# A hybrid decoder step: who makes the low halves of the weights, a new order of the mixer steps, and gate rows spread in one pass

## The reference

```python
u = _rmsnorm(h, w['norm1_g']) @ w['w_in']           # all mixer inputs in one product
y_a, ... = _rglru(a_x, a_g, ...)                    # causal conv, two sigmoid gates, linear recurrence
y_b = _swa_prompt(q, k, v, w['attn_sinks'])         # window of 128; a cached version for the samples
y_c, ... = _hgrn2(c_q, c_f, c_i, c_g, lb, s0, ...)  # chunks of 64, decay for every key channel
y_d, ... = _mlstm(d_q, d_k, d_v, d_o, d_i, d_f, ...)  # chunks of 64, gates of one number a head
h = h + jnp.concatenate([y_a, y_b, y_c, y_d], axis=-1) @ w['w_out']
f = _rmsnorm(h, w['norm2_g']) @ w['w_up']
h = h + jnp.square(jax.nn.relu(f)) @ w['w_down']
h = h + jax.nn.sigmoid(h @ w['w_ple_gate']) * (p_l @ w['w_ple_proj'])
```

## Time and profile before

| | us |
|---|---|
| median of 3 runs | 2978.51 |
| lowest, highest | 2973.07, 2979.11 |
| the profiled execution | 2969.13 |
| its span in the profile | 2966.9 |
| TensorE busy | 2818.4 (95%) |
| GpSimd busy | 1440.4 (49%) |
| VectorE busy | 1347.5 (45%) |
| ScalarE busy | 1114.2 (38%) |
| mean granted clock of TensorE | 0.975 |

### The profile page before, as it was taken

One profiled execution on the slowest core, in us unless ns is written; L12 is line 12 of the kernel. 1 busy time (PEld: TensorE's weight loads), 2 busy tenths in 40 slices (PEclk: granted clock), 3 DMA queues, 4 the chain that ended last, 5 costly groups with the idle time before them and its releaser, 6 DMA issues.

```text
span 2966.9 us, 43775 instructions
## 1 busy us (share of the span) xinstructions
PE 2818.4 (95%) x17944; PEld 2495.7 (84%) x17944; DVE 1347.5 (45%) x2398; ACT 1114.2 (38%) x1728; POOL 1440.4 (49%) x896
## 2 busy tenths in 40 slices
PE   7998998899989999999999899999999999999998
PEld 6878776677867898989998887878789779999998
DVE  6647346556645545435442266544453423222222
ACT  5442334542333444433332344533333243322222
POOL 3336333445734744446642554434664265555453
PEclk9999999999999999999998999999999899999999
DMA  4322222332232432222222242323222234233232
GB/s 163 111 86 65 86 73 78 109 104 82 79 102 80 136 106 79 85 78 85 81 80 63 72 150 79 107 66 100 85 85 81 65 91 153 93 93 93 92 94 86
DMA packets 85717, 274.20 MB, mean 92 GB/s; under 512 B 9994, under 2 KB 10762, under 8 KB 85520
## 3 DMA queue, kind: packets, MB, share of 16 engines
q1 hardware_dynamic: 71312, 243.23, 26.3%
q10 hardware_dynamic: 14208, 28.18, 2.7%
HBM read 251.31 MB, written 20.06 MB: 91 GB/s over the span
## 4 chain that ended last, share of the span: by engine, by line
PE 78%; DVE 6%; POOL 4%; ACT 3%; issue 2%; DMA 1%; ACTq 0%; SPq 0%; DVEq 0%; POOLq 0%
PE pj L644 23%; PE pj L646 23%; PE pj L645 23%; POOL w_lo L1559 2%; DVE sl L1656 2%; PE pm L728 1%; PE pm L912 1%; POOL m_lo L1629 1%; ACT w_hi L1072 1%; PE pm L993 1%; DMA out_y<-res 1%; PE pm L1012 1%; PE pm L820 1%; DVE wide L2091 0%; PE pm L832 0%
## 5 line engine op out<-in xcount | busy, mean ns | idle before, releaser
L1559 POOL TENSOR_TENSOR w_lo<-w_raw,w_hi 128x1024 fp32r<-128x1024 f32 x428 | 1051.3, 2460 | 1038.5 <-ACT w_hi L1072 1038.0
L644 PE MATMUL pj<-m_hi,w_hi 128*128 128x260 f32 (+1 forms) x2320 | 748.0, 322 | 18.1 <-POOL w_lo L1559 7.5
L646 PE MATMUL pj<-m_hi,w_lo 128*128 128x260 f32 (+1 forms) x2320 | 732.6, 316 | 0.0
L645 PE MATMUL pj<-m_lo,w_hi 128*128 128x260 f32 (+1 forms) x2320 | 732.3, 316 | 0.0
L644 PE MATMUL pj<-hid,w_hi 128*128 128x260 f32 (+1 forms) x1920 | 631.0, 329 | 21.0 <-POOL hid L1622 9.9
L646 PE MATMUL pj<-hid,w_lo 128*128 128x260 f32 (+1 forms) x1920 | 622.3, 324 | 0.0
L1072 ACT ACTIVATE w_hi<-w_raw 128x1024 fp32r<-128x1024 f32 x428 | 447.7, 1051 | 394.9 <-PE pj L646 373.7
L645 PE MATMUL pj<-hid,w_hi 128*128 128x260 f32 (+1 forms) x1536 | 496.6, 323 | 0.0
L644 PEld LDWEIGHTS pj<-m_hi,w_hi 128*128 128x128 f32 x2320 | 442.4, 191 | 55.5 <-POOL w_lo L1559 12.9
L645 PEld LDWEIGHTS pj<-m_lo,w_hi 128*128 128x128 f32 x2320 | 441.7, 190 | 31.5 <-issue 3.4
L646 PEld LDWEIGHTS pj<-m_hi,w_lo 128*128 128x128 f32 x2320 | 441.7, 190 | 28.8
(11 more groups left out here) (318 smaller groups left out, 3254.4 us busy)
## 6 DMA issues: line engine op xcount, KB each, us to landing
w_raw<-in_w SPq DMA_DIRECT2D x428, 512.0 KB, 3.5
out_e<-stage SPq DMA_DIRECT2D x23, 260.0 KB, 3.8
sl<-out_e SPq DMA_DIRECT2D x23, 260.0 KB, 4.0
out_y<-res ACTq DMA_DIRECT2D x16, 260.0 KB, 4.6
out_y<-res ACTq DMA_DIRECT2D x16, 256.0 KB, 4.6
x_b<-in_x SPq DMA_DIRECT2D x4, 520.0 KB, 13.7
res<-in_x ACTq DMA_DIRECT2D x8, 260.0 KB, 4.7
res<-out_y ACTq DMA_DIRECT2D x8, 260.0 KB, 5.4
```

What stands on the lines that cost most here:

```text
L644: pe.matmul(out, wh, hi[:, k, c0:c1], start=(k == 0), stop=False)
L645: pe.matmul(out, wh, lo[:, k, c0:c1], start=False, stop=False)
L646: last = pe.matmul(out, wl, hi[:, k, c0:c1], start=False, stop=(k == n - 1))
L1559: pool.tensor_tensor(w_lo[:, j % RAW_BUFS, :], w_raw[:, j % RAW_BUFS, :], w_hi[:, j % HI_BUFS, :].bitcast(F32), ALU.subtract).then_inc(lo_ ...
```

## The change

1. **Low parts.** Of the 428 tiles, 390 get their `w_lo` on VectorE and 38 on GpSimd (the 32 tiles of `wout`, and three after `gates` in q = 2 and 3). `lo_made` becomes two semaphores, one per engine.
2. **hgrn levels.** `q_diag` is dropped; the levels are multiplied in place, six operations a chunk on VectorE instead of twelve, and every level is four products of K = 64.
3. **Rows and conv of pass 1** are done beside the output products of pass 0 (`BESIDE`), with slots of their own; their loads come earlier. The reciprocal is replaced by a short polynomial on VectorE.
4. **Steps.** A gate step becomes two (one for each half of the channels), so there are four in a pass; `hdiag` comes after both `hprep` 2 and 3 and in pass 0 has two dense steps of the next pass ahead of it; one `AFTER` entry moves from `mc` 0 to `mc` 3. `_sequence` now holds products back until dense steps worth 1.0 have passed (`down` counts 0.5).
5. **vt** uses another PSUM bank for v = 2 and 4; the table of `rope` is loaded after the step's products.
6. **Gate rows in `mc`.** VectorE writes the rounded rows to partitions 64 to 67 and the remainder to 96 to 99 of `grow`; one F32R product over 36 partitions with a selector `gsel` spreads their sum.

The core of the diff:

```diff
@@ _sequence
+        if late and x[0] not in ('sq', 'resid'):
+            out, held, late = out + held, [], False
...
         elif x[0] in DENSE:
-            out, held = out + [(x, 'dense')] + held, []
+            out.append((x, 'dense'))
+            passed += 0.5 if x[0] == 'down' else 1.0
+            late = passed >= 1.0
         else:
-            out, held = out + held + [(x, 'pre')], []
+            out, held, passed = out + held + [(x, 'pre')], [], 0.0
@@ which engine makes a low part
+    by_pool = {JOBS[x][0] for x in JOBS if x[0] == 'wout'}
+    for q in (2, 3):
+        first = JOBS[('job', q, 'gates')][0]
+        by_pool |= set(range(first + 2, first + 5))
@@ vector, at the end of each dense step
+                    dve.wait_ge(hi_made, j + 1)
+                    dve.tensor_tensor(w_lo[:, j % RAW_BUFS, :], w_raw[:, j % RAW_BUFS, :],
+                                      w_hi[:, j % HI_BUFS, :].bitcast(F32), ALU.subtract).then_inc(lo_made[0], 1)
...
+                if part == 'dense':
+                    split_lo(JOBS[x][-1] + 3)
@@ rows
-                    link(dve.tensor_scalar(t2, t2, -1.0, 1e-30, ALU.add, ALU.max))
-                    link(dve.reciprocal(t2, t2))
+                    link(dve.tensor_scalar(t2, t2, -0.5, 1.5, ALU.mult, ALU.add))
+                    link(tt(f, f, t2, ALU.mult))
+                    link(tt(ln, ln, f, ALU.subtract))
...
+                    link(dve.tensor_copy(f[:, 0:HALF].bitcast(F32R), ig[:, 0:HALF]))
+                    dve.tensor_copy(grow[64:68, 0:HALF], ig[:, 0:HALF])
+                    dve.tensor_tensor(grow[96:100, 0:HALF], ig[:, 0:HALF], f[:, 0:HALF], ALU.subtract).then_inc(rows_v, 1)
@@ mc, tensor
-                        last = pe.matmul(pm[:, 0, i * CH:(i + 1) * CH], ident[0:4, head:head + 1].to_broadcast([4, P]),
-                                         rows8[0:4, cc], start=False, stop=(i == 3), skip_group_check=True)
+                        last = pe.matmul(pm[:, 0, i * CH:(i + 1) * CH], gsel[64:100, head:head + 1].to_broadcast([36, P]),
+                                         grow[64:100, cc], start=False, stop=(i == 3), skip_group_check=True)
@@ hP, tensor: every level
-                            if l < 6:
-                                out = pm[:, bank + j, :].rearrange("p (h s) -> p h s", h=2)[:, :, at:at + 64]
-                                last = pe.matmul(out, el[:, j, :], q_diag[:, l % 4, j], start=True, stop=True)
-                                continue
                             for hh in range(2):
                                 r = slice(64 * hh, 64 * hh + 64)
-                                last = pe.matmul(pm[:, bank + hh, j * 256 + at:j * 256 + at + 64], el[r, j, :],
-                                                 el[r, j, half:], start=True, stop=True)
+                                last = pe.matmul(pm[:, bank + hh, j * 256 + at:j * 256 + at + 64], el[r, j, :], odd[r, j],
+                                                 start=True, stop=True)
```

More of the change, by code:

```diff
@@ L81, in mixer @@
     if ahead:
-        o = take(q, 'gates', 'ag0', 'ag1') + [('rows', q, 0), ('rows', q, 1)]
+        o = [('rowsT', q)] + take(q, 'ag0', 'ag1')
     else:
@@ L156, in blend @@
     return out + ff
-AFTER = {('rows', 1): 2, ('conv', 0, 1): 2, ('conv', 1, 1): 2, ('gate', 0): 1, ('gate', 1): 1, ('rows', 5): 2, ('lru', 1): 2,
+AFTER = {('rows', 1): 2, ('hdiag',): 2, ('conv', 1, 1): 2, ('gate', 0, 1): 1, ('gate', 1, 1): 1, ('rows', 5): 2, ('lru', 1): 2,
          ('rowsT',): 2, ('rope', 2): 2, ('ropeE', 1): 1, ('rot', 0): 1, ('rot', 2): 1, ('attn', 0): 2, ('attn', 1): 2,
@@ L179, in _order @@
     for q in range(4):
-        ahead = [('load', 1, 'ax0'), ('load', 1, 'ax1')] + [('conv', 1, j, n) for j in range(2) for n in range(2)]
         for n in range(KT):
-            o += [('wout', q, n)] + ([ahead[n]] if q == 0 and n < 6 else [])
-        o += blend(mixer(q + 1), feed(q), 3) if q < 3 else feed(q)
+            o += [('wout', q, n)] + (BESIDE[n] if q == 0 else [])
+        ff = feed(q)
+        first = ff.index(('up', q, 0, 2)) if q == 0 else 0
+        o += ff[:first] + blend(mixer(q + 1), ff[first:], 3) if q < 3 else ff
         o += [('pload', q)]
@@ L194, in _sequence @@
 def _sequence():
-    out, held = [], []
+    out, held, passed, late = [], [], 0.0, False
     for x in ORDER:
+        if late and x[0] not in ('sq', 'resid'):
+            out, held, late = out + held, [], False
         if x[0] in AUX:
@@ L244, in _tables @@
         if part == 'pe':
[L245 to L253, removed]
+            if what in ('gate', 'gnorm', 'rope', 'rot', 'norm1', 'norm2'):
+                for name in [x + (i,) for i in range(2)] if what == 'gnorm' else [x]:
+                    mixes[name] = m
+                    m += n
     return shot, job, used_until, mixes
@@ L758, in gate @@
             def gate(x):
[L759 to L762, removed]
+                q, g, j = x[1:]
+                pe.wait_ge(conv_v, 2 * q + j + 1)
+                mix(MIX[x], q, pc(q // 2, 'wr' if g == 0 else 'wi', j * P, P), slot(11 + j))
             def rope(x):
@@ L1176, in gate @@
             def gate(x):
[L1177 to L1180 removed]
+                q, g, j = x[1:]
+                take_mix(MIX[x], q, slot(13 + 2 * g + j), ACT.Sigmoid, bias=pc(q // 2, 'br' if g == 0 else 'bi', j))
             def lru(x):
@@ L2000, in hprep @@
                     last.then_inc(hp_v, 1)
-            def diagonal(lev, qs):
-                for hh in range(2):
-                    r = slice(64 * hh, 64 * hh + 64)
-                    last = tt(q_diag[r, lev % 4, :, hh, :].rearrange("p j (n b) -> p j n b", b=1 << lev),
-                              halves(level(lev)[r], lev)[1], halves(qs[r], lev)[1], ALU.mult)
-                return last
             def hE(x):
@@ L2032, in hE @@
                     dve.wait_ge(hc_exp, 3 * n + g)
-                    for lev in ((0, 1), (2, 3))[g - 1]:
-                        last = diagonal(lev, qs)
+                    for lev in GROUPS[g - 1]:
+                        e1 = halves(level(lev), lev)[1]
+                        last = tt(e1, e1, halves(qs, lev)[1], ALU.mult)
                     last.then_inc(hc_kq, 1)
```

147 lines of the change are left out of this document (90 added, 57 removed).

## The result

| | before | with the change |
|---|---|---|
| median, us | 2975.79 (4 runs) | 2952.88 (4 runs) |
| lowest, highest | 2972.55, 2979.11 | 2949.51, 2957.22 |
| the profiled execution, its span | 2969.13, 2966.9 | 2952.48, 2950.7 |

The direction and the range held; the gain is less than half of the forecast one.

A forecast was written before the change was run, and what follows sets the result against it. TensorE's matmuls were taken as the floor (busy 2818.4 of 2966.9 us). Gains of 71.5 less costs of 26 gave net -45.5: 2923.6 from the profiled execution, 2933 from the median, middle 2928; range 2878 to 2971.

The forecast's parts named there:

- The low parts: 390 of 428 low parts move from GpSimd to VectorE: 11 us less of TensorE's waits for w_lo.
- the price of VectorE's queue: VectorE, working in order, makes low parts late for the next dense tile: three waits, +8 us (0 to 25).
- The slow rival: VectorE's in-order queue is late with low parts, so TensorE waits for w_lo: slower, 3012 us; chance 0.10.
- The rival of the shared path: VectorE and GpSimd still hold each other up on shared memory access: only 9 us gained, 2969; chance 0.14.
- gates, hdiag and vt: TensorE's waits in gate steps, hdiag and vt shrink by reordering and another PSUM bank: -12, -6 and -3 us.
- four new waits: Last half's hdiag, sattn and rope lack a dense product between preparation and products: about 2 us each, +8 (0 to 16).
- The hgrn waits: Waits for VectorE's copies in the hgrn levels (13.8 + 4.7 us) halve as its work is less stretched: -9 (0 to -18).
- The products of the levels: In the hgrn levels, four K = 64 products replace pairs of K = 128: +5 us over 96 levels (-1 to +14).
- The spread: Spreading the gate rows in one F32R pass saves about 0.45 us, 16 times: -7 us (-9 to 0).
- The rows beside the output products: Some 22 row operations, about 16 us, on VectorE beside the first output products barely fit: +5 us (0 to 12).
- Hid: TensorE's waits for hid, 9.9 us, left unchanged because GpSimd had waited for ScalarE's hsq, not for a low part.
- The clock: Four half-clock stretches at hdiag, gate and m_lo waits end when those waits go: -13 us (0 to -19).

## Why the prediction was wrong in size

*The low parts: right on the engines, and the step that failed is the price of VectorE's queue.* GpSimd's 518 us and VectorE's 1568 fit, and so does the 1.27 us; m_lo fell by 2.7 of the forecast 5, mden and stage by 3.0 of 5.5. The forecast put the cost of the in-order queue where the low part is needed, at the next dense tile (+8, "with all of the next mixer step behind it"), and left attention at nothing, "since they end on ScalarE or on a chain within the step". The move by itself did not lengthen the waits for w_lo: 15.9 us in the kernel with the low parts alone, where the terms come to 15. But VectorE is a part of that chain within the attention step, at the place shown it has no gap, and a low part that it makes there delays the chain, by up to its own length. The attention waits rose from 13.1 to 20.2 us, and to 27.5 with the low parts alone; the runs with and without those 30 or 32 tiles give 14 and 24 us.

*The slow rival named the right queue, but not the right wait.* It priced VectorE's queue in waits for w_lo; what was late was the attention's work behind the low part. In the kernel with the low parts alone this took back the whole gain: ratio 1.0. The rival of the shared path falls: moving 390 low parts is worth 14 us in the new order and, without the attention's, 24 in the old one. The page of the Trainium skill that was cited for it ("Perfetto Trace Analysis", section "Optimizing Scalar/DVE Operations") says "might not help"; the engines do collide here (2.77 against 0.75 us), but the move did help, in the old order as long as the attention's stayed on GpSimd. It took most of the collisions away: with the low parts alone VectorE is busy 1620.1 us, where its 1347.5 before and the 495.5 of the 390 low parts add to 1843, so 223 us of its other work were stretching.

*Order: gates, hdiag and vt came near the forecast; the rope step was priced far too low.* The sigmoid line fell by 11.5 (forecast 12), less 1.9 that now wait in the gate step for the conv; hdiag by 4.5 (6), its longest wait growing from 3.0 to 4.1; vt from 3.7 to 1.0 (3). The forecast had the rope step among four new waits of about 2 us (+8, 0 to 16), for want of a dense product in between. The issue of the rope table behind the loads was in the diff, and had no term: +14.4 us of waits, 18 with the clock. The waits for w_lo that did grow in the changed kernel came with the order as well, 8.0 us of them at the first output products and the `up` step behind them.

*The hgrn waits* fell by 11.8 (9 forecast), but in the new order not through the relief, as the run with all low parts on GpSimd shows; the prediction had the multiplication in place "off the path". The products of the levels cost about 2 us more over all chunks by the starts of their steps, within the bounds of +5. *The spread* gave 9.8 us directly, where the forecast had 7, and 9 with the low clock counted; in all it was worth 20 with what went through the clock. *The rows beside the output products* cost 9, within 0 to 12 and by the late evictions that were named.

*Hid* was left at 9.9 and fell to 2.4. It stands at 9.9 with the low parts alone, at 2.4 with all of them on GpSimd in the new order, and at 12.5 with the old rule for held products: the rule did it. *Two lines without a term* grew: evictions (`res`) from 4.5 to 7.3, and the mLSTM chunks' wait for `wide` (L1044) from 4.3 to 8.3. Both are at least as long with all low parts on GpSimd (15.0 and 8.3), so they too belong to the order.

*The clock* was to give 13 and gave 0 in the profiles. Of the stretches that were named, those of the gate step, of m_lo and of hdiag at 1321.7 are gone, and the first one of hdiag has shrunk from 10.2 us to about 3. Others came: 10.2 and 6.8 behind the rope step, some 10 at the output products, about 7 in the per-layer stage of half 1 behind waits of 2.66 and 2.72 for VectorE's low parts, and 10 instead of 3 at the last hdiag. The forecast priced the end of old stretches only, not the start of new ones behind its own new waits.

## What to carry to other kernels

When work moves to an engine that runs in order, price it at what stands behind it in that queue, and look first for stretches in which the engine is the chain: there a moved piece can cost its whole length, and leaving those few pieces where they were can be worth as much as moving all the others. When a transfer's issue is moved, write down every other issue on that queue that it passes. And a saved wait saves clock only if no new wait takes its place.

## What the runs showed of the hardware

The issue of one transfer held ScalarE's instruction stream for 9.23 and 9.13 us (passes 1 and 3) when two loads had been issued on the same queue 4 us before, and for 0.56 and 0.57 us when it stood ahead of them. VectorE's work ran shorter when GpSimd no longer made the low parts beside it: 223 us less of the same instructions. The one-pass product on 36 partitions took as long for each record (320 ns, overlapped) as the fp32 one on 4 (321 ns). And an edit that takes 9.8 us out of products, and one that only shifts products behind a further dense step, moved the time by 20 and 19 us, of which, by the mean granted clocks, some 11 and 14 went with the low clock.
